# FFN way up: a weight's high part times both parts of x in one 512-column matmul, the halves added on the way out of PSUM

## The reference, cut to what matters

```
def _conv_ffn(h, w_up, conv_w, conv_b, w_down):            # FFN 0
    u = _causal_dwconv(h @ w_up, conv_w, conv_b)           # all 5632 columns
    a, b = jnp.split(u, 2, axis=-1)
    return (jax.nn.gelu(a) * b) @ w_down

def conv_ffn(x, w_up, conv_w, conv_b, w_down):             # FFN 1, 2
    a, g = jnp.split(x @ w_up, 2, axis=-1)
    g = lax.conv_general_dilated(g, conv_w[:, None, :], ...) + conv_b   # 2816 columns
    return (jax.nn.gelu(g) * a) @ w_down
```

## Time and profile before

| | us |
|---|---|
| runs | 1397.16, 1405.97, 1407.62; median 1405.97 |
| the profiled execution | 1404.47 |
| its span, first to last instruction | 1403.2 |
| PE busy | 1306.4 (93%) |
| DVE busy | 891.0 (63%) |
| ACT busy | 590.7 (42%) |
| matmuls of the ways up, L1599 (3024 and, of the first units, 144) | 367.6 and 18.1 |
| matmuls of the ways down, L1612 and L1627 | 168.9 and 17.1 |

### The profile page before, as it was taken

How to read it: one execution, slowest core, us unless ns; L and a number is a source line. 1 busy time by engine, 2 the same in 40 slices (tenths; PEclk the granted TensorE clock), 3 DMA queues, 4 the chain that set the end, 5 groups by cost and what they waited for, 6 DMA issues and landing times. The chain is left out here.

```text
span 1403.2 us, 21127 instructions
## 1 busy us (share of the span) xinstructions
PE 1306.4 (93%) x8537; PEld 1189.0 (85%) x8537; DVE 891.0 (63%) x1257; ACT 590.7 (42%) x900; POOL 119.7 (9%) x152
## 2 busy tenths in 40 slices
...
GB/s 284 148 122 146 138 150 149 122 133 134 119 128 197 186 182 182 124 151 181 91 2 150 151 185 193 192 211 82 117 142 175 59 1 92 124 195 191 181 210 61
DMA packets 178589, 202.75 MB, mean 144 GB/s; under 512 B 21868, under 2 KB 163147, under 8 KB 178492
## 3 DMA queue, kind: packets, MB, share of 16 engines
...
HBM read 200.30 MB, written 1.08 MB: 144 GB/s over the span
## 5 line engine op out<-in xcount | busy, mean ns | idle before, releaser
L1316 DVE TENSOR_TENSOR w_parts<-raw,w_parts 128x1024 fp32r<-128x1024 f32 (+1 forms) x268 | 333.8, 1245 | 166.8 <-ACT w_parts L1305 159.0
L1305 ACT CAST w_parts<-raw 128x1024 fp32r<-128x1024 f32 (+1 forms) x268 | 279.3, 1042 | 331.6 <-PE ps L1599 103.4
L1599 PEld LDWEIGHTS ps<-hT_parts,w_parts 128*128 128x128 f32 x3024 | 366.6, 192 | 2.1
L1599 PE MATMUL ps<-hT_parts,w_parts 128*128 128x256 f32 x3024 | 367.6, 283 | 0.0
L1612 PE MATMUL ps<-w_parts,gT_parts 128*128 128x512 f32 x720 | 168.9, 390 | 0.0
L1612 PEld LDWEIGHTS ps<-w_parts,gT_parts 128*128 128x128 f32 x720 | 133.3, 188 | 26.4
L1365 PE MATMUL ps<-w_parts,hT_parts 128*128 128x256 f32 (+1 forms) x864 | 116.9, 302 | 16.7 <-DVE w_parts L1316 12.1
L1365 PEld LDWEIGHTS ps<-w_parts,hT_parts 128*128 128x128 f32 x864 | 115.6, 212 | 18.2 <-DVE w_parts L1316 12.5
L1363 PE MATMUL ps<-hT_parts,w_parts 128*128 128x256 f32 x912 | 119.4, 296 | 8.4 <-DVE w_parts L1316 4.5
L1363 PEld LDWEIGHTS ps<-hT_parts,w_parts 128*128 128x128 f32 x912 | 118.0, 205 | 9.9 <-DVE w_parts L1316 5.1
L458 PE MATMUL ps<-hT,ring 128*128 128x256 f32 x448 | 98.6, 380 | 1.0 <-DVE hT L310 1.0
...
## 6 DMA issues: line engine op xcount, KB each, us to landing
raw<-in_ffn_w_up SPq DMA_DIRECT2D x44, 1024.0 KB, 5.1
raw<-in_f_w_up SPq DMA_DIRECT2D x22, 1024.0 KB, 5.1
raw<-in_ffn_w_down SPq DMA_DIRECT2D x22, 1024.0 KB, 5.1
ring<-in_w_in SPq DMA_DIRECT2D x18, 1024.0 KB, 5.5
raw<-in_ev_w_in SPq DMA_DIRECT2D x15, 1024.0 KB, 5.4
raw<-in_f_w_down SPq DMA_DIRECT2D x11, 1024.0 KB, 4.8
ring<-in_x_wkv SPq DMA_DIRECT2D x8, 1024.0 KB, 5.4
ring<-in_w_out SPq DMA_DIRECT2D x4, 1024.0 KB, 5.2
```

Source lines behind the costliest of these rows:

```text
L1305: self.done(A, A.copy(high[:, c], self.raw[:, u % RAW, c]), self.s_hi)
L1316: self.done(V, V.tensor_tensor(low[:, c], self.raw[:, u % RAW, c], high[:, c].bitcast(F32), ALU.subtract), self.s_lo)
L1599: mm = T.matmul(self.ps[:, b, m * 256:m * 256 + 256], w[:, kk, m * P:(m + 1) * P], x[:, kk, :], start=kk == 0 and q == 0, stop=kk == KD - ...
```

## The change

For each block of inputs and each half of the columns, the weight's high part now meets both parts of x in one matmul of 512 columns, since the two parts lie side by side in `hT_parts`. It writes a whole bank: high x high in columns 0 to 255, high x low in 256 to 511. A second matmul, of 256 columns, adds low x high to the second half. A way up is 32 matmuls and takes two banks: 4 and 5 for every a(i), 6 and 7 for every b(i).

The two halves of a bank must be added. ACT copies the first halves of both banks to a new place in SBUF (`act_up`, COPY 128 x 512), DVE adds the second halves to that (`dve_up`, TENSOR_TENSOR 128 x 512) and thereby frees the banks. The conv instructions now read this sum from SBUF; ACT's wait for `dve_up` instead of for PE. In FFN 1 and 2 the gate takes b from there too.

The order of the units' end changes: ... b(8) d(7) a(9) b(9) a(10) b(10) d(8) d(9) d(10). ACT's splits of the last two units stand behind the gate's high part of step 10, which waits for d(8).

```diff
             add("a", 1)
-            for i in range(1, FI):
+            for i in range(1, FI - 2):
                 add("b", i)
                 add("d", i - 1)
-                if i < FI - 1:
-                    add("a", i + 1)
-            add("d", FI - 1)
+                add("a", i + 1)
+
+            for n, i in (("b", FI - 2), ("a", FI - 1), ("b", FI - 1), ("d", FI - 3), ("d", FI - 2), ("d", FI - 1)):
+                add(n, i)
...
         self.g32 = [self.place(at + 2048 + 512 * p, 2, SEQ) for p in range(2)]
+        self.up = {"a": self.place(at + 3072, 2, SEQ), "b": self.place(at + 3584, 2, SEQ)}
...
     def pe_up(self, n, i, ready=None):
+
         T, u = self.T, self.ff[n, i]
-        b = 4 + 2 * (i % 2) + (n == "b")
+        b = 6 if n == "b" else 4
         wh, wl = self.pe_parts(u)
-        self.take(b)
-        xh, xl = self.hparts
+        self.take(b, b + 1)
         for m in range(2):
             for kk in range(KD):
                 if ready is not None:
                     self.pe_ready(ready, range(NT), kk)
-                for q, (w, x) in enumerate(((wh, xh), (wh, xl), (wl, xh))):
-                    mm = T.matmul(self.ps[:, b, m * 256:m * 256 + 256], w[:, kk, m * P:(m + 1) * P], x[:, kk, :],
-                                  start=kk == 0 and q == 0, stop=kk == KD - 1 and q == 2)
-        self.ff_fills[n, i] = self.filled(mm, b, by=self.s_unit)
+                T.matmul(self.ps[:, b + m, :], wh[:, kk, m * P:(m + 1) * P], self.hTr[:, :, kk, :], start=kk == 0, stop=False)
+                mm = T.matmul(self.ps[:, b + m, 256:512], wl[:, kk, m * P:(m + 1) * P], self.hTr[:, 0, kk, :],
+                              start=False, stop=kk == KD - 1)
+        self.ff_fills[n, i] = self.filled(mm, b, also=(b + 1,), by=self.s_unit)
...
     def act_ffn(self, cols):
...
-        for i in range(1, FI):
+        for i in range(1, FI - 1):
             self.act_split(self.ff["b", i] + 1)
+            self.act_up("a", i)
             self.act_conv("a", i, cols)
-            self.act_split(self.ff["d", i - 1] + 1)
+            self.act_split(self.ff["b", i] + 2)
+            self.act_up("b", i)
             self.act_conv_b(i, cols)
-            if i < FI - 1:
-                self.act_gelu(i)
-                self.act_split(self.ff["a", i + 1] + 1)
-                self.act_high(i)
-            else:
-                self.act_gate(i)
-        self.act_split(self.ff["d", FI - 1] + 1)
+            self.act_gelu(i)
+            if i < FI - 2:
+                self.act_split(self.ff["b", i] + 3)
+            self.act_high(i)
+        i = FI - 1
+        self.act_split(self.ff["b", i] + 1)
+        self.act_up("a", i)
+        self.act_conv("a", i, cols)
+        self.act_split(self.ff["b", i] + 2)
+        self.act_up("b", i)
+        self.act_conv_b(i, cols)
+        self.act_gelu(i)
+
+        self.A.wait_ge(*self.unit_done(self.ff["d", FI - 3]))
+        self.act_high(i)
+        self.act_split(self.ff["d", i])
+        self.act_split(self.ff["d", i] + 1)
         self.act_ask(ACT.Sqrt)
 
+    def act_up(self, n, i):
+
+        A, f = self.A, self.ff_fills[n, i]
+        A.wait_ge(*self.full(f))
+        self.done(A, A.copy(self.up[n], self.ps[:, f[0]:f[0] + 2, 0:256]), self.s_up)
+
     def act_conv(self, n, i, cols):
 
-        A, f, y = self.A, self.ff_fills[n, i], self.y[i % 2][n == "b"]
-        A.wait_ge(*self.full(f))
+        A, y = self.A, self.y[i % 2][n == "b"]
+        A.wait_ge(*self.drained(self.ff_fills[n, i]))
         if i >= 2:
             A.wait_ge(*self.gated(i - 2))
-        bank = self.bank2(f)
         for m in range(2):
-            ins = A.activation(y[:, m, :], bank[:, m, :], ACT.Identity, bias=cols("b", n, 2 * i + m), scale=cols(2, n, 2 * i + m))
+            ins = A.activation(y[:, m, :], self.up[n][:, m, :], ACT.Identity, bias=cols("b", n, 2 * i + m), scale=cols(2, n, 2 * i + m))
...
     def dve_ffn(self, cols):
...
         for i in range(1, FI):
             self.dve_split(self.ff["b", i] + 1)
+            self.dve_up("a", i)
             self.dve_conv("a", i, cols)
-            self.dve_split(self.ff["d", i - 1] + 1)
+            self.dve_split(self.ff["b", i] + 2)
+            self.dve_up("b", i)
             self.dve_conv_b(i, cols)
...
+    def dve_up(self, n, i):
+
+        V, f, u = self.V, self.ff_fills[n, i], self.up[n]
+        V.wait_ge(*self.s_up.next("V"))
+        self.drain(V, V.tensor_tensor(u, u, self.ps[:, f[0]:f[0] + 2, 256:512], ALU.add), f)
+
     def dve_conv(self, n, i, cols):
...
-                ins = V.scalar_tensor_tensor(y[:, m, d:SEQ], bank[:, m, 0:SEQ - d], cols(tap, n, 2 * i + m), y[:, m, d:SEQ],
+                ins = V.scalar_tensor_tensor(y[:, m, d:SEQ], u[:, m, 0:SEQ - d], cols(tap, n, 2 * i + m), y[:, m, d:SEQ],
                                              ALU.mult, ALU.add)
```

More of the change, by code:

```diff
@@ L112, in __init__ @@
         self.s_affine, self.s_affine_x = sem("s_affine_done"), sem("s_affine_dve")
-        self.s_tap, self.s_gelu, self.s_prod, self.s_ghi, self.s_g = sem("s_tap"), sem("s_gelu"), sem("s_product"), sem("s_g_high"), sem("s_gated")
+        self.s_up = sem("s_up_high")
+        self.s_tap, self.s_taps, self.s_gelu, self.s_prod = sem("s_tap"), sem("s_earlier_taps"), sem("s_gelu"), sem("s_product")
+        self.s_ghi, self.s_g = sem("s_g_high"), sem("s_gated")
         self.s_max, self.s_tb, self.s_final, self.s_zero = sem("s_row_max"), sem("s_table"), sem("s_final_norm"), sem("s_zeros")
@@ L1580, in pe_ffn @@
         self.pe_up("a", 1)
-        for i in range(1, FI):
+        for i in range(1, FI - 2):
             self.pe_up("b", i)
             self.pe_down(i - 1)
-            if i < FI - 1:
-                self.pe_up("a", i + 1)
+            self.pe_up("a", i + 1)
+        self.pe_up("b", FI - 2)
+        self.pe_up("a", FI - 1)
+        self.pe_up("b", FI - 1)
+        self.pe_down(FI - 3)
+        self.pe_down(FI - 2)
         self.pe_down_last()
@@ L1633, in act_ffn @@
         self.act_split(self.ff["a", 0] + 1)
+        self.act_up("a", 0)
         self.act_split(self.ff["b", 0] + 1)
         self.act_conv("a", 0, cols)
+        self.act_up("b", 0)
         self.act_split(self.ff["a", 1] + 1)
@@ L1676, in act_gelu @@
         y = self.y[i % 2][0]
-        self.A.wait_ge(*self.drained(self.ff_fills["a", i]))
+        self.A.wait_ge(*self.s_taps.next("A"))
         self.done(self.A, self.A.activation(y, y, ACT.Gelu_apprx_tanh), self.s_gelu)
     def act_high(self, i):
[L1683 to L1686, removed]
+        self.A.wait_ge(*self.s_prod.next("A"))
         self.done(self.A, self.A.copy(self.gTr[:, i % 2, 0], self.g32[i % 2]), self.s_ghi)
@@ L1699, in dve_ffn @@
         self.dve_split(self.ff["a", 0] + 1)
+        self.dve_up("a", 0)
         self.dve_split(self.ff["b", 0] + 1)
         self.dve_conv("a", 0, cols)
+        self.dve_up("b", 0)
         self.dve_split(self.ff["a", 1] + 1)
@@ L1706, in dve_ffn @@
             self.dve_split(self.ff["b", i] + 1)
+            self.dve_up("a", i)
             self.dve_conv("a", i, cols)
-            self.dve_split(self.ff["d", i - 1] + 1)
+            self.dve_split(self.ff["b", i] + 2)
+            self.dve_up("b", i)
             self.dve_conv_b(i, cols)
-            if i < FI - 1:
-                self.dve_split(self.ff["a", i + 1] + 1)
+            if i < FI - 2:
+                self.dve_split(self.ff["b", i] + 3)
             self.dve_gate(i)
@@ L1714, in dve_ffn @@
                 self.dve_affine(i - 1)
+        self.dve_split(self.ff["d", FI - 1])
         self.dve_split(self.ff["d", FI - 1] + 1)
+    def dve_up(self, n, i):
+        V, f, u = self.V, self.ff_fills[n, i], self.up[n]
+        V.wait_ge(*self.s_up.next("V"))
+        self.drain(V, V.tensor_tensor(u, u, self.ps[:, f[0]:f[0] + 2, 256:512], ALU.add), f)
     def dve_conv(self, n, i, cols):
-        V, f, y = self.V, self.ff_fills[n, i], self.y[i % 2][n == "b"]
-        bank = self.bank2(f)
+        V, u, y = self.V, self.up[n], self.y[i % 2][n == "b"]
         V.wait_ge(*self.s_tap.next("V"))
@@ L1723, in dve_conv @@
             for d, tap in ((1, 1), (2, 0)):
-                ins = V.scalar_tensor_tensor(y[:, m, d:SEQ], bank[:, m, 0:SEQ - d], cols(tap, n, 2 * i + m), y[:, m, d:SEQ],
+                ins = V.scalar_tensor_tensor(y[:, m, d:SEQ], u[:, m, 0:SEQ - d], cols(tap, n, 2 * i + m), y[:, m, d:SEQ],
                                              ALU.mult, ALU.add)
-                if m == 1 and d == 2:
-                    self.drain(V, ins, f)
+                if m == 1 and d == 2 and n == "a":
+                    self.done(V, ins, self.s_taps)
                 else:
```

10 lines of the change are left out of this document (2 added, 8 removed).

## The result

The changed kernel takes 1417.76 us (median of 9 runs, 1411.41 to 1423.24), the one before 1405.31 (9 runs): a ratio of 1.0097, 95% interval 1.0077 to 1.0116. It is 1% slower, as forecast. The profiled execution took 1416.77 us.

The account below looks back on a forecast made before the run. PE bounded the FFNs before; after the change a DVE and ACT chain bounds FFN 0, PE still FFN 1 and 2. 1404.5 + 18.8 (FFN 0) - 5.8 (FFN 1 and 2) = 1417.5 us, range 1408 to 1426.

Parts of the forecast that it names:

- The fewer matmuls: Ways up on PE: 5.76 us becomes 5.57, 0.19 less each; 12.7 us over 66 if PE stays the bound.
- The new work: Per way up: DVE addition 0.69 us, ACT copy 0.59, ACT conv pair 1.23, four DVE taps 2.03.
- Rival 2: DVE's taps are cheaper from SBUF, 425 ns for 483, saving 4.4 us in FFN 0: 1412.5 us; chance 0.10.
- The ring of FFN 0: DVE and ACT wait in a closed chain of 18.53 us per step, above PE's 16.61; FFN 0 18.8 us longer.
- Rival 1: PE bounds everywhere because FFN 0's chain is not closed; faster, 1394 us; chance 0.07.
- FFN 1 and 2: PE stays the bound; each -4.2 + 2.0 - 0.65 = -2.9 us, both 5.8 us shorter.
- The waits by the new order: PE waits in FFN 1 and 2 at the end, plus some 0.5 in the first step: 2.0 us each.
- the 0.65 of before: PE's wait in FFN 1 and 2 of the kernel before, 0.65 us each, forecast to go.
- Rival 4: FFN 1 and 2's slack missing (4.8 us, total 1422), or 1.2 GHz after d(10) wait (5.5 us); chance 0.10.
- The sum: Whole kernel: 1404.5 + 18.8 - 5.8 = 1417.5 us.
- Rival 3: The wide matmul saves nothing; FFN 1 and 2 lose their 4.2 us each: 1426 us; chance 0.07.

Follow-up runs that it names:

- e6: Changed kernel with the 8 wide matmuls of each half of a way up first, then the 8 narrow ones; 1418.03 us (one execution).
- e2: Changed kernel with ACT's copy and DVE's addition ahead of the weight split in each step, for both halves; 1393.12 us, ratio to before 0.992.
- e3: Changed kernel with DVE's addition done twice in FFN 0, once to a spare place; 1438.62 us (one execution).
- e10: Changed kernel with copy and addition ahead of the split for half a(i) only, b(i) left behind its split; 1398.06 us (one execution).
- e1: Changed kernel with the two parts of x side by side per block of inputs, one piece for the wide matmul; 1419.15 us, ratio to before 1.0108.
- e8: The kernel before, unchanged, profiled a second time; 1398.34 us (one execution); FFN 1 lost 0.44 us per us at the lower clock.

## Why the prediction was right

**The fewer matmuls**: 0.19 us per way up forecast, 0.115 measured (5.76 - 5.65). The term was too large, by the 5 ns a pair that alternating costs. e6 gets the full 0.19 by running each form in a block. In FFN 1 and 2 this is 44 x 0.08 = 3.5 us. The Trainium skill's page "TensorE: Matmul & The Clock Gate", section "Back-to-back issue gap", gives 2.5 ns of fixed cost for an isolated matmul. That is not the price here, where a weight load goes with every matmul: a matmul less gave 7 ns when alternating (0.115 / 16) and 12 in blocks.

**The new work**: 0.69, 0.59, 1.24 and 2.04 us against 0.69, 0.59, 1.23 and 2.03. Rival 2 falls: the tap took 484 ns from SBUF. The 65 ns that the Trainium skill's "Perfetto Trace Analysis", section "Optimizing Scalar/DVE Operations", has VectorE save on SBUF do not show in this operation. For ScalarE it has SBUF 42 ns dearer, and with that the conv's 36 (602 for the 566 from PSUM) roughly agree.

**The ring of FFN 0**: 18.53 us forecast, 18.53 measured. PE's waits in a step are 0.54 us before a(i) and 0.79 before b(i), forecast 0.8 and 1.1; PE needs 16.79 us a step and not 16.61, which leaves less to wait. The addition of step 9 came at 561.1, forecast 562.4, and PE had begun 1.7 earlier in this execution; from there to d(10) it is 32.0 us, forecast 32.1. Without the slow d(10), 1.4 us, FFN 0 is 19.2 longer; forecast 18.8. e2, e3 and e10 show that it is a ring: it shrinks by what is taken off it until PE sets the pace, and it grows by what one puts in. Rival 1 falls with it.

**FFN 1 and 2**: forecast 2.9 us shorter each, measured 0.15 shorter and 0.14 longer. Three things are in that. The alternation takes 1.75 each. The clock was at its lower level for 3.1 and 3.4 us near their beginning, by 0.44 us per us some 1.4 and 1.5; in e1 and e3 FFN 2 had none of this and took 186.5 and 186.3, 1.3 to 1.5 under before. The waits by the new order, 2.0 forecast, come to 2.05 to 2.25 if the difference of these to e2's 184.25 is put down to them (in e2's FFN 2 PE has no wait of 0.15 us or more behind the first), and the 0.65 of before is gone. That 184.25 is itself 0.3 us under the sum of the terms (187.75 - 22 x 0.115 - 0.65), and this rest stays open. Rival 4, the missing slack in the middle steps, falls: in the middle steps PE does not wait, in e6 neither, where it runs at the rate of the forecast (step 16.61). Its other part, a lower clock behind the long wait before d(10), did come, at 1.4 us and not 5.5.

**The sum** came out at 1417.5 for 1417.8 (the profiled execution: 1416.8), closer than its parts deserve, and that is luck. With e8's 0.44 the 9.9 us of lower clock in the three FFNs of the profile cost 4.4; 20.6 - 4.4 = 16.2 is what the change does, against 13.0 forecast, and the 3.5 of the alternation close the gap to 0.3. In the pair of profiles the rest was made up by 8.4 us elsewhere, in which the clock was at its lower level for 23 us less (102.5 for 125.5). In the medians, 12.5 us with an interval of 10.8 to 16.3, and 15.2 for e1, there is room for 16. Rival 3 was the nearest to having a part: the wide matmul saved less than the rows said, though not nothing.
